# Hybrid decoder step: half tiles of the gated unit and the third head unit change places in the head recurrence

## The chip, the cores and the metric

One core of one Trainium2 chip runs the kernel, one inference step of a small decoder. The metric is device time in microseconds (us), the median of the runs. The engines are TensorE (PE: matmuls; PEld is its loading of weights), VectorE (DVE), ScalarE (ACT), GpSimd (POOL) and SyncE (SP). SP and POOL issue the transfers; SP's queue streams the weights into a ring of seven slots.

## What is computed

Two layers. Each projects its normalized input, runs two token mixers beside each other, merges them and ends in a feed-forward part: dense in the first layer, a mixture of eight experts in the second. The change lies in the mixers:

```python
# branch A: diagonal complex scan y, then a gated linear unit
out = (y @ w_glu1) * jax.nn.sigmoid(y @ w_glu2)
# branch B: for 8 heads, a matrix state s over the tokens
def step(s, inp):
    r_t, w_t, k_t, v_t, kk_t, a_t = inp
    sa = jnp.einsum('bhvk,bhk->bhv', s, -kk_t)
    s = (s * w_t[:, :, None, :] + sa[..., None] * (kk_t * a_t)[:, :, None, :]
         + v_t[..., None] * k_t[:, :, None, :])
    return s, jnp.einsum('bhvk,bhk->bhv', s, r_t)
# merge, then the feed-forward part
m = sigmoid(g_a) * A + sigmoid(g_b) * B
x = x + m @ w_out
```

There are 272 prompt tokens (one sequence) and 8 single-token samples with a state of their own.

## The kernel before

All activations lie with features on the partitions, 280 columns (272 prompt tokens, 8 samples). The recurrence of branch B isn't run token by token: the prompt is cut into a first piece of 16 tokens (the "head" steps, names with s_) and four chunks of 64. A **unit** is a pair of chunks for half of the heads: units 0 and 1 serve chunks 0 and 1, units 2 and 3 chunks 2 and 3. A unit's steps run in a fixed order: gram, square, quad_, oct_, e8, m_, m2, q_, inv. They build the inverse of a 64x64 triangular matrix per head by repeated squaring; each is a set of 64x64 products on PE into two PSUM banks of the unit's own (2u and 2u + 1), read out by ACT or DVE before the next step can start. When both units of a pair are done, the **chunk steps** follow, one chunk after the other: chunk_in (product with the state at the chunk's start), a DVE addition, chunk_solve (product with the inverse), a copy on ACT and one on DVE, chunk_state (the new state), a DVE addition. Then outputs(l, 0) or outputs(l, 1) makes the outputs of the pair.

The **samples** need one step of the recurrence: samples_in (128 products with two columns each), samples_rows (rows into two banks, turned), samples_dot, then samples_spread on DVE and samples_state on PE and DVE, one for each of four head pairs.

The **gated unit** has 8 tiles of 128 features. A tile n is a gate half, glu_half(l, n, 1), with a sigmoid on ACT (glu_gate), and a value half, glu_half(l, n, 0); DVE multiplies both into the merge gate (glu_out). A half is four 128x128 products with 280 columns into bank 4 (the first gate half: bank 5). The half tiles don't depend on the recurrence and stand between its steps.

The order is written out by hand, three times: rwkv(l) of the tensor engine (L914), of ACT (L1482) and of DVE (L2102). Each engine works through its list, with semaphore waits inside the steps. The lists start with the gated unit's first half tiles and units 0 and 1; unit 3 starts beside their end; unit 2 starts at gram(l, 2), between the steps of the first pair's chunks (it waits until all eight tiles of the gated unit are done, because its banks are 4 and 5). The last six half tiles (tiles 5, 6, 7) stand ahead of chunk_state(l, 0).

finish_rwkv(l) (L1005) waits until both pairs' outputs (o_out) and the samples' states (so_out) are done, gives seven ring slots back to SP, and normalizes the outputs; from there on the layer is a chain up to the feed-forward part. POOL stores the samples' states when so_out has reached its last count.

Names in the code: pools[i] is PSUM bank i; room(l, u, i) a buffer of unit u; mm (L447) issues every matmul, fn (L1282) every ACT operation, so the profile's lines for these two engines are always the same, and steps are told apart by shape, count and time. Of DVE's lines, L2047 is chunk_in, L2053 chunk_solve, L2059 chunk_state, L2066 outputs, L2011 the additions of the unit steps, L2093 samples_spread, L2099 samples_state, L1937 and L1939 glu_out.

## Time and profile before

| | us |
|---|---|
| median of 3 runs | 2017.32 |
| lowest and highest | 2012.21, 2017.56 |
| the profiled execution, its own time | 2021.26 |
| span in the profile | 2019.5 |
| PE busy | 1931.4 (96%) |
| DVE busy | 1342.5 (66%) |
| ACT busy | 978.1 (48%) |

The profile is of one execution. Busy shares are means over stages with different limits: the experts, the last half of the span, are dense on PE, while the mixers have stretches in which PE waits. A row of the timeline gives start, length, engine, line, operation, operands (out<-in, with buffers by name: "arena", "ring" and "s" are SBUF, "bank" is PSUM), the count of merged instructions, and in brackets the idle time before and what ended it. The ends of matmuls are modelled, so two neighbouring rows can overlap; starts are exact. A product in 32-bit floats is two matmul instructions. The granted clock is a share of 2.4 GHz, the higher of two levels; the lower is 1.2 GHz.

For the two layers, the stage between the change's first and last step is cut into A (six half tiles among unit steps), a short stretch around chunk_in(0), C (unit and chunk steps without half tiles), D (from the samples' products to the end of unit 2) and E (the second pair's chunks, up to the first sums of finish_rwkv).

### The profile page before, as it was taken

To read this page: it belongs to the slowest core of one execution; us is meant where nothing else is said; L and a number is where in the kernel's file an instruction comes from. 1 tells how busy PE (TensorE), PEld (TensorE's weight loads), DVE (VectorE), ACT (ScalarE), POOL (GpSimd) and SP (SyncE) were. 2 spreads that over 40 slices of the span, in tenths; PEclk is the share of its full clock that TensorE was granted. 3 is DMA by queue.
4 is the path that set the end of the run, shared out by engine and by line. 5 is a ranking of instruction groups with operands and counts; after the bars stand their busy time and mean duration, and the time that the engine had idled before them with its cause. 6 is when DMAs were issued, how large, how long until landed. Compare 5 with 4: busy or idle time off the path is not lost.

```text
span 2019.5 us, 34327 instructions
## 1 busy us (share of the span) xinstructions
PE 1931.4 (96%) x14001; PEld 1600.4 (79%) x14001; DVE 1342.5 (66%) x1479; ACT 978.1 (48%) x957; POOL 44.9 (2%) x40
## 2 busy tenths in 40 slices
PE   8999998899999999998699999999999999999997
PEld 6876885799987777876588787887878878788775
DVE  7484344445534384353478888988888888888885
ACT  2232321344321213220377767768677776767763
POOL 0000000000000000000000000000000000000000
PEclk9989997999999899988699999999999999999998
DMA  8534005344443451015299999999999999999982
GB/s 333 140 67 89 2 3 211 137 172 175 174 139 112 106 97 54 2 57 198 85 346 378 356 377 353 365 380 358 371 366 372 367 362 377 360 368 365 407 333 86
DMA packets 69949, 474.75 MB, mean 235 GB/s; under 512 B 8721, under 2 KB 9905, under 8 KB 14617
## 3 DMA queue, kind: packets, MB, share of 16 engines
q1 hardware_dynamic: 64800, 451.33, 60.3%
q0 software_dynamic: 4736, 20.74, 3.7%
q8 instruction: 86, 1.41, 0.3%
q10 hardware_dynamic: 304, 1.08, 0.1%
q14 instruction: 23, 0.18, 0.0%
HBM read 463.92 MB, written 11.37 MB: 235 GB/s over the span
## 4 chain that ended last, share of the span: by engine, by line
PE 46%; ACT 2%; DVE 1%; DMA 1%; issue 1%; DVEq 0%; ACTq 0%; SPq 0%
PE bank L447 44%; ACT w_hi L1282 1%; PE bank L1235 1%; DMA ring<-wstream_dram 1%; PE bank L1161 0%; ACT he_hi L1282 0%; DVE he_lo L2297 0%; DVE w_lo L2344 0%; DMA arena<-tokens_dram,token_i 0%; PE bank L1171 0%; DVE arena L2291 0%; DVE arena L1687 0%; DVE x L2310 0%; DVE rstd L1685 0%; DVE y_lo L2304 0%
## 5 line engine op out<-in xcount | busy, mean ns | idle before, releaser
L2344 DVE TENSOR_TENSOR w_lo<-ring,w_hi 128x2048 fp32r<-128x2048 f32 x336 | 754.9, 2284 | 42.4 <-ACT w_hi L1282 41.1
L1282 ACT ACTIVATE w_hi<-ring 128x2048 fp32r<-128x2048 f32 x336 | 626.1, 1911 | 38.7 <-DMA ring<-wstream_dram 37.9
L447 PE MATMUL bank<-arena,ring 128*128 128x280 f32 (+1 forms) x1856 | 441.8, 401 | 18.9 <-DVE arena L1914 7.9
L447 PEld LDWEIGHTS bank<-arena,ring 128*128 128x128 f32 (+1 forms) x1856 | 341.4, 195 | 105.0 <-issue 21.4
L1282 ACT ACTIVATE arena<-bank 128x280 f32<-128x280 f32 (+8 forms) x292 | 131.7, 468 | 583.3 <-PE bank L447 550.3
L447 PE MATMUL bank<-w_hi,he_hi 128*128 128x512 f32 x896 | 361.8, 404 | 9.0 <-DVE he_lo L2297 8.5
L447 PE MATMUL bank<-w_lo,he_hi 128*128 128x512 f32 x896 | 354.1, 395 | 0.0
L447 PE MATMUL bank<-w_hi,he_lo 128*128 128x512 f32 x896 | 353.4, 394 | 0.0
L447 PEld LDWEIGHTS bank<-w_hi,he_hi 128*128 128x128 f32 x896 | 169.0, 189 | 50.2 <-issue 11.9
L447 PEld LDWEIGHTS bank<-w_hi,he_lo 128*128 128x128 f32 x896 | 168.9, 189 | 41.4
L447 PEld LDWEIGHTS bank<-w_lo,he_hi 128*128 128x128 f32 x896 | 169.4, 189 | 35.9
L447 PE MATMUL bank<-w_hi,at_hi 128*128 128x512 f32 x448 | 177.8, 397 | 0.4 <-DVE w_lo L2344 0.4
L447 PE MATMUL bank<-w_hi,at_lo 128*128 128x512 f32 x448 | 177.0, 395 | 0.0
L447 PE MATMUL bank<-w_lo,at_hi 128*128 128x512 f32 x448 | 175.2, 391 | 0.0
L447 PE MATMUL bank<-arena 64*64 64x64 f32 (+14 forms) x3920 | 160.4, 250 | 11.5 <-ACT arena L1282 5.4
L447 PEld LDWEIGHTS bank<-arena 64*64 64x64 f32 (+7 forms) x3920 | 135.2, 142 | 38.0 <-issue 19.0
L1680 DVE TENSOR_TENSOR w_lo<-ring,fw_hi 128x2048 fp32r<-128x2048 f32 x33 | 75.6, 2292 | 51.2 <-ACT fw_hi L1282 51.2
L447 PE MATMUL bank<-h_hi,fw_hi 128*128 128x280 f32 x352 | 104.0, 295 | 5.1 <-DVE h_lo L2182 5.1
L447 PE MATMUL bank<-h_lo,fw_hi 128*128 128x280 f32 x352 | 103.5, 294 | 0.0
L447 PE MATMUL bank<-h_hi,w_lo 128*128 128x280 f32 x352 | 103.3, 293 | 0.0
L447 PEld LDWEIGHTS bank<-w_hi,at_lo 128*128 128x128 f32 x448 | 84.1, 188 | 19.5
L447 PEld LDWEIGHTS bank<-w_lo,at_hi 128*128 128x128 f32 x448 | 84.3, 188 | 19.2
(276 smaller groups left out, 1783.4 us busy)
## 6 DMA issues: line engine op xcount, KB each, us to landing
ring<-wstream_dram SPq DMA_DIRECT2D x427, 1024.0 KB, 6.7
parts_dram<-zeros_dram POOLq DMA_DIRECT2D x1, 2112.0 KB, 14.0
s<-s_dram POOLq DMA_DIRECT2D x2, 1024.0 KB, 14.4
o_rw_dram<-s POOLq DMA_DIRECT2D x2, 1024.0 KB, 4.9
arena<-parts_dram POOLq DMA_DIRECT2D x2, 1024.0 KB, 11.7
x<-x_dram SPq DMA_DIRECT2D x2, 560.0 KB, 4.3
y_dram<-arena SPq DMA_DIRECT2D x4, 280.0 KB, 2.1
arena<-s_b_dram POOLq DMA_DIRECT2D x2, 512.0 KB, 6.3
```

The source lines that it names most:

```text
L447: return nc.tensor.matmul(out, lhsT, rhs, start=start, stop=stop, **k)
L1235: last = nc.tensor.transpose(pools[2][:, b * P:(b + 1) * P], act_e[:, b * P:(b + 1) * P], ident[:])
L1282: return nc.scalar.activation(out, in_, func, **k)
L1680: v.tensor_tensor(w_lo[(FFN_AT + n) % RING], slot(FFN_AT + n), fw_hi[n % 4].bitcast(F32), ALU.subtract)\
L2344: v.tensor_tensor(w_lo[n % RING], slot(n), w_hi[n % HALVES].bitcast(F32), ALU.subtract)\
```

## The change

The third unit (unit 2) starts earlier, beside unit 3, with its steps between those of unit 3 and the first pair's chunks. The last six half tiles of the gated unit go behind: between the chunk steps of the second pair. Since unit 2 uses bank 4 before they run, they go to bank 3, and the first of them waits until ACT has read outputs(l, 0) out of that bank. samples_rows then can't use bank 3 and runs in two parts through bank 1, the second part after ACT has read the first. The last two samples_state steps go behind outputs(l, 1). gram(l, 2) waits for five tiles of the gated unit, not eight. On DVE the decay of the samples' states is cut into two halves. The number of products and of elementwise operations is the same.

```diff
@@ -61,2 +61,3 @@
 HELD = 4
+GLU_LATE = 5
 
@@ -327,2 +328,5 @@
 
+        def glu_bank(n, c):
+            return 3 if n >= GLU_LATE else 5 if n == 0 and c else 4
+
         def quad(bank, n):
@@ -567,5 +571,7 @@
                 s = MIX_AT[l] + S_WIN + n // 2
-                bank = 5 if n == 0 and c else 4
+                bank = glu_bank(n, c)
                 if n == 0 and c:
                     pe.wait_ge(S["bonus_out"], l + 1)
+                if n == GLU_LATE and c:
+                    pe.wait_ge(S["o_act"], 4 * l + 2)
                 if c:
@@ -709,3 +715,3 @@
                     pe.wait_ge(S["tok_out"], 6 * l + 6)
-                    pe.wait_ge(S["glu_out"], DC * (l + 1))
+                    pe.wait_ge(S["glu_out"], DC * l + GLU_LATE)
                 if u_ == 3:
@@ -884,10 +890,13 @@
 
-            def samples_rows(l):
+            def samples_rows(l, i):
 
-                pe.wait_ge(S["sm_out"], l + 1)
-                pe.wait_ge(S["o_act"], 4 * l + 2)
-                for j, (bank, row) in enumerate(((1, 0), (1, 32), (3, 0), (3, 32))):
+                if i == 0:
+                    pe.wait_ge(S["sm_out"], l + 1)
+                    pe.wait_ge(S["o_act"], 4 * l + 2)
+                else:
+                    pe.wait_ge(S["smt_out"], 2 * l + 1)
+                for j, row in enumerate((0, 32)):
                     for f in range(CB):
-                        src = (sm[:, f, :, 0], z[:, 8 + f, TP:T], beta_e[:, f, TP:T], chi_e[:, f, TP:T])[j]
-                        last = mm(pools[bank][row:row + NS, f * P:(f + 1) * P], src, ident[:])
+                        src = (sm[:, f, :, 0], z[:, 8 + f, TP:T], beta_e[:, f, TP:T], chi_e[:, f, TP:T])[2 * i + j]
+                        last = mm(pools[1][row:row + NS, f * P:(f + 1) * P], src, ident[:])
                 last.then_inc(S["smt_ps"], 1)
@@ -903,3 +912,3 @@
                 if f == 0:
-                    pe.wait_ge(S["smt_out"], l + 1)
+                    pe.wait_ge(S["smt_out"], 2 * l + 2)
                 elif f == 1:
@@ -952,53 +961,54 @@
                 token_rows(l, 1, 1)
-                glu_half(l, 5, 1)
                 m_(l, 1)
                 m2(l, 0)
-                quad_(l, 3)
                 token_rows(l, 1, 2)
-                glu_half(l, 5, 0)
+                quad_(l, 3)
                 m2(l, 1)
                 q_(l, 0)
+                gram(l, 2)
                 oct_(l, 3)
-                glu_half(l, 6, 1)
                 q_(l, 1)
                 inv(l, 0)
+                square(l, 2)
                 e8(l, 3)
-                glu_half(l, 6, 0)
                 inv(l, 1)
+                quad_(l, 2)
                 m_(l, 3)
-                glu_half(l, 7, 1)
                 chunk_in(l, 0)
+                oct_(l, 2)
                 m2(l, 3)
-                glu_half(l, 7, 0)
                 chunk_solve(l, 0)
+                e8(l, 2)
                 q_(l, 3)
-                gram(l, 2)
                 chunk_state(l, 0)
+                m_(l, 2)
                 inv(l, 3)
                 chunk_in(l, 1)
-                square(l, 2)
-                chunk_solve(l, 1)
-                quad_(l, 2)
-                chunk_state(l, 1)
-                oct_(l, 2)
-                outputs(l, 0)
-                e8(l, 2)
-                samples_in(l)
-                m_(l, 2)
-                samples_rows(l)
                 m2(l, 2)
-                samples_dot(l)
+                chunk_solve(l, 1)
                 q_(l, 2)
+                chunk_state(l, 1)
                 inv(l, 2)
-                samples_state(l, 0)
+                outputs(l, 0)
                 chunk_in(l, 2)
-                samples_state(l, 1)
+                samples_in(l)
+                glu_half(l, 5, 1)
                 chunk_solve(l, 2)
-                samples_state(l, 2)
+                glu_half(l, 5, 0)
                 chunk_state(l, 2)
+                samples_rows(l, 0)
+                glu_half(l, 6, 1)
                 chunk_in(l, 3)
-                samples_state(l, 3)
+                samples_dot(l)
+                samples_rows(l, 1)
+                glu_half(l, 6, 0)
                 chunk_solve(l, 3)
+                glu_half(l, 7, 1)
+                samples_state(l, 0)
                 chunk_state(l, 3)
+                glu_half(l, 7, 0)
+                samples_state(l, 1)
                 outputs(l, 1)
+                samples_state(l, 2)
+                samples_state(l, 3)
 
@@ -1408,3 +1418,3 @@
                 ac.wait_ge(S["glu_ps"], DC * l + n + 1)
-                fn(glu_s[:, n % 2, :], pools[4 if n else 5][:, 0:T], ACT.Sigmoid).then_inc(S["glu_sig"], 1)
+                fn(glu_s[:, n % 2, :], pools[glu_bank(n, 1)][:, 0:T], ACT.Sigmoid).then_inc(S["glu_sig"], 1)
 
@@ -1473,8 +1483,8 @@
 
-            def samples_rows(l):
-                ac.wait_ge(S["smt_ps"], l + 1)
+            def samples_rows(l, i):
+                ac.wait_ge(S["smt_ps"], 2 * l + i + 1)
                 ac.wait_ge(S["smt_zero"], l + 1)
-                for bank, out in ((1, out_r(l)), (3, out_l)):
-                    for row in (0, 32):
-                        ins = fn(out[row:row + NS], pools[bank][row:row + NS, :].rearrange("p (f a v) -> p f a v", f=CB, a=2), ACT.Identity)
+                out = (out_r(l), out_l)[i]
+                for row in (0, 32):
+                    ins = fn(out[row:row + NS], pools[1][row:row + NS, :].rearrange("p (f a v) -> p f a v", f=CB, a=2), ACT.Identity)
                 ins.then_inc(S["smt_out"], 1)
@@ -1509,29 +1519,30 @@
                 token_rows(l, 1, 1)
-                glu_gate(l, 5)
                 m_(l, 1)
-                quad_(l, 3)
                 token_rows(l, 1, 2)
+                quad_(l, 3)
                 q_(l, 0)
                 oct_(l, 3)
-                glu_gate(l, 6)
                 q_(l, 1)
                 inv(l, 0)
+                square(l, 2)
                 inv(l, 1)
+                quad_(l, 2)
                 m_(l, 3)
-                glu_gate(l, 7)
+                oct_(l, 2)
                 chunk_solve(l, 0)
                 q_(l, 3)
+                m_(l, 2)
                 inv(l, 3)
-                square(l, 2)
                 chunk_solve(l, 1)
-                quad_(l, 2)
-                oct_(l, 2)
-                outputs(l, 0)
-                samples_in(l)
-                m_(l, 2)
-                samples_rows(l)
                 q_(l, 2)
                 inv(l, 2)
+                outputs(l, 0)
+                samples_in(l)
+                glu_gate(l, 5)
                 chunk_solve(l, 2)
+                samples_rows(l, 0)
+                glu_gate(l, 6)
+                samples_rows(l, 1)
                 chunk_solve(l, 3)
+                glu_gate(l, 7)
                 outputs(l, 1)
@@ -1938,3 +1949,3 @@
                 dve.wait_ge(S["glu_value_ps"], DC * l + n + 1)
-                v.tensor_tensor(gate[:, n, :], gate[:, n, :], pools[4][:, 0:T], ALU.mult).then_inc(S["glu_out"], 1)
+                v.tensor_tensor(gate[:, n, :], gate[:, n, :], pools[glu_bank(n, 0)][:, 0:T], ALU.mult).then_inc(S["glu_out"], 1)
 
@@ -2073,4 +2084,7 @@
                 tt(sm_r[:, 1], chi_e[:, :, TP:T], z[:, 0:4, TP:T], ALU.mult).then_inc(S["sm_dot_in"], 1)
+
+            def samples_decayed(l, fs):
+                tt = v.tensor_tensor
                 dve.wait_ge(S["sm_ps"], l + 1)
-                for f in range(CB):
+                for f in fs:
                     tt(s0[:, f], s0[:, f], wend[:, f, 1 + NCH:].unsqueeze(2).broadcast_to([P, NS, N]), ALU.mult)
@@ -2088,3 +2102,3 @@
             def samples_spread(l, f):
-                dve.wait_ge(S["smt_out"], l + 1)
+                dve.wait_ge(S["smt_out"], 2 * l + 1)
                 if f >= 2:
@@ -2125,5 +2139,5 @@
                 quad_(l, 3)
-                glu_out(l, 5)
                 m2(l, 1)
                 q_(l, 0)
+                gram(l, 2)
                 oct_(l, 3)
@@ -2131,38 +2145,40 @@
                 e8(l, 3)
-                glu_out(l, 6)
+                quad_(l, 2)
                 m_(l, 3)
                 chunk_in(l, 0)
+                oct_(l, 2)
                 m2(l, 3)
-                glu_out(l, 7)
                 chunk_solve(l, 0)
+                e8(l, 2)
                 q_(l, 3)
-                gram(l, 2)
                 chunk_state(l, 0)
+                m_(l, 2)
                 chunk_in(l, 1)
+                m2(l, 2)
                 chunk_solve(l, 1)
-                quad_(l, 2)
+                q_(l, 2)
                 chunk_state(l, 1)
-                oct_(l, 2)
-                e8(l, 2)
                 outputs(l, 0)
-                m_(l, 2)
                 samples_ready(l)
-                m2(l, 2)
-                samples_dot(l)
-                q_(l, 2)
+                chunk_in(l, 2)
+                samples_decayed(l, (0, 1))
+                chunk_solve(l, 2)
+                glu_out(l, 5)
+                chunk_state(l, 2)
+                samples_decayed(l, (2, 3))
                 samples_spread(l, 0)
+                chunk_in(l, 3)
+                samples_dot(l)
                 samples_spread(l, 1)
+                glu_out(l, 6)
+                chunk_solve(l, 3)
                 samples_state(l, 0)
-                chunk_in(l, 2)
                 samples_spread(l, 2)
+                chunk_state(l, 3)
+                glu_out(l, 7)
                 samples_state(l, 1)
-                chunk_solve(l, 2)
                 samples_spread(l, 3)
-                chunk_state(l, 2)
+                outputs(l, 1)
                 samples_state(l, 2)
-                chunk_in(l, 3)
                 samples_state(l, 3)
-                chunk_solve(l, 3)
-                chunk_state(l, 3)
-                outputs(l, 1)
```

## Rows read from the trace of the kernel before

**Rows 1.** Windows, layer 0: stretch, busy time by engine, granted clock, DMA share, GB/s.
```profile
243.58:266.05 22.47, 22.47 (x399) 18.97 (x398) 6.83 (x17) 5.99 (x13) 0.00 (x0) 1.00 0.01 2
...
270.02:284.31 14.29, 13.50 (x415) 13.29 (x415) 6.67 (x17) 3.18 (x8) 0.00 (x0) 1.00 0.01 3
...
284.31:299.88 15.57, 14.72 (x299) 13.23 (x295) 8.10 (x22) 4.51 (x10) 0.00 (x0) 0.78 0.01 2
...
299.88:316.57 16.69, 14.44 (x240) 10.90 (x240) 10.21 (x20) 2.23 (x5) 1.45 (x2) 0.80 0.21 74
```

**Rows 2.** The windows view, layer 1: the last three of the same stretches.
```profile
857.44:871.73 14.29, 13.50 (x414) 13.29 (x415) 6.67 (x17) 3.18 (x8) 0.00 (x0) 1.00 0.01 3
...
871.73:885.58 13.85, 13.05 (x300) 11.32 (x296) 8.29 (x22) 4.51 (x10) 0.00 (x0) 0.88 0.02 4
...
885.58:903.33 17.75, 15.47 (x241) 12.26 (x241) 10.23 (x20) 2.27 (x5) 1.45 (x2) 0.71 0.20 68
```

**Rows 3.** Waits of weight loads, D and E: us, times, longest; both layers.
```profile
PEld bank L447 <- DVE arena L2047: 2.2, 2, 1.2
...
PEld bank L447 <- DVE ring L2093: 0.8, 2, 0.6
...
PEld bank L447 <- DVE ring L2059: 0.7, 1, 0.7
...
PEld bank L447 <- DVE arena L2011: 0.6, 2, 0.4
...
PEld bank L447 <- DVE arena L2047: 1.9, 2, 1.0
...
PEld bank L447 <- DVE arena L2011: 0.4, 1, 0.4
```

**Rows 4.** The same view of A to C, layer 0.
```profile
PEld bank L447 <- DVE ring L2059: 0.9, 1, 0.9
```

**Rows 5.** Windows of 5 us around the samples' products, both layers.
```profile
280.00:285.00 5.00, 5.00 (x188) 5.00 (x182) 1.76 (x5) 1.39 (x4) 0.00 (x0) 1.00 0.01 3
...
285.00:290.00 5.00, 5.00 (x119) 5.00 (x118) 0.77 (x2) 0.04 (x1) 0.00 (x0) 0.63 0.01 3
...
875.00:880.00 5.00, 5.00 (x93) 4.13 (x93) 2.42 (x7) 0.82 (x2) 0.00 (x0) 0.68 0.02 3
```

**Rows 6.** The timeline of PE: start, length, operation, count, idle before.
```profile
243.69 2.05 PE L447 MATMUL bank<-arena,ring 128*128 128x280 f32 x8
...
818.54 3.84 PE L447 MATMUL bank<-arena,ring 128*128 128x280 f32 x8
...
284.45 5.15 PE L447 MATMUL bank<-arena,s 64*64 64x2 f32 x122
...
871.88 3.76 PE L447 MATMUL bank<-arena,s 64*64 64x2 f32 x123
```

**Rows 7.** The timeline of ACT, layer 0: reads of chunk_solve(3) and of outputs(1).
```profile
309.99 0.38 ACT L1282 ACTIVATE arena<-bank 64x256 f32<-64x256 f32 x1 [6.03 <-PE bank L447]
...
315.08 0.66 ACT L1282 ACTIVATE arena<-bank 128x256 f32<-128x256 f32 x2 [4.71 <-PE bank L447]
```

**Rows 8.** Timeline: sigmoid of the sixth gate half; product with its value half.
```profile
245.84 0.40 ACT L1282 ACTIVATE arena<-bank 128x280 f32<-128x280 f32 x1 [1.35 <-PE bank L447]
...
252.60 0.45 DVE L1939 TENSOR_TENSOR arena<-arena,bank 128x280 f32<-128x280 f32 x1 [1.68 <-PE bank L447]
```

**Rows 9.** The timeline around the end of the stage, layer 0.
```profile
308.49 0.69 DVE L2099 TENSOR_TENSOR s<-s,bank 128x512 f32<-128x512 f32 x1 [0.56 <-PE bank L447]
...
315.77 0.69 DVE L2066 TENSOR_TENSOR arena<-arena,bank 128x512 f32<-128x512 f32 x1 [3.63 <-ACT arena L1282]
...
316.60 4.46 PE L447 MATMUL bank<-arena,blk 128*128 128x280 f32 x14 [1.57 <-DVE arena L2066]
...
329.87 17.40 PE L447 MATMUL bank<-arena,ring 128*128 128x280 f32 x64 [3.97 <-DVE arena L1914]
```

**Rows 10.** The page, part 6: one DMA issue.
```profile
o_rw_dram<-s POOLq DMA_DIRECT2D x2, 1024.0 KB, 4.9
```

44 lines of the change are left out of this document (22 added, 22 removed).

## The prediction

> **What bounds the kernel now.** The edit touches one stage only, the head recurrence, once in each of the two layers. I cut that stage into stretches with the windows view and asked of each how long it is, how busy TensorE (PE) is and which clock it is granted [rows 1, 2]. The reader is to see three things. In the first stretch (A, with six half tiles of the gated unit between the unit steps) PE never rests and the granted clock is 1.00, that is 2.4 GHz. In C (unit and chunk steps alone) it is still 1.00, with a short rest. In D and E (samples, then the second pair of chunks) the mean granted clock falls to 0.78 and 0.80 in layer 0 and to 0.88 and 0.71 in layer 1. So the stage is bound by PE's own program order: the timeline shows its steps one behind the other as rwkv writes them, and what PE waits for, or does at 1.2 GHz, is paid in full.
>
> Next I read the waits of PE's weight loads, which start at the moment a wait ends and so show stalls that the modelled ends of matmuls cover [rows 3, 4]. In D and E named waits are 2.2 + 0.8 + 0.7 + 0.6 = 4.3 us in layer 0 and 1.9 + 0.8 + 0.7 + 0.4 = 3.8 us in layer 1 (the two rows at 0.8 and 0.7 read the same there), all for VectorE (DVE): chunk 2 and chunk 3 are a chain of chunk_in, solve and state with a DVE or ScalarE (ACT) step after each, and the order gives PE next to nothing to do between them. In A to C there is one such wait, 0.9 us, in front of the second chunk. The "issue" waits of at most 0.3 us are the ordinary change from one kind of step to another, and stay.
>
> Third, the clock. The first fall comes with the samples' products (64x2): PE is busy 5.00 of 5.00 us both in the slice before and in the slice in which the clock drops to 0.63, and layer 1 shows the same at 0.68 [rows 5]. So it isn't idleness that brings this fall. The second fall is in E, where PE stops and starts between the chunk steps. What the lower level does to a step is seen in like rows: a half tile takes 2.05 us at 2.4 GHz and 3.84 at 1.2, and the samples' products 3.76 and 5.15, the latter only partly at the lower level [rows 6].
>
> **The change, part by part.** All PE work is kept: the same half tiles, unit steps, chunk steps and sample products. What changes is what lies between what.
>
> *Six half tiles leave A, unit 2 takes their place.* This costs nothing if each unit step still has cover for its hand-over. A hand-over is about 0.1 us from the last product to the reader and 0.4 for the reader [rows 8], estimated at 0.5 to 0.8 in all with wider reads. Products of the 64x64 kind go at the rate of 3.76 us for 123, or 31 ns [rows 6], so a step of 32 to 48 covers 1.0 to 1.5 us. In the new order nearly every step of units 2 and 3 has at least 32 products of other work before its successor; the tightest are square(2) to quad_(2) (behind e8(3) and inv(1)) and m_(2) to m2(2) (behind inv(3) and chunk_in(1)), 32 products each, and m2(2) to q_(2), behind the 16 of chunk_solve(1) alone. I take 0.4 us of stalls a layer; the bounds are 0 and the whole of the cover gone (a rival, below). The 0.9 us wait in front of chunk_in(1) goes: it came from five DVE operations of gram(2) queued ahead of chunk_state(0), and gram(2) now lies long before.
>
> *Six half tiles go between the second pair's chunk steps.* Each is 2.05 us, and the longest wait there is 1.2. So the named waits of D and E go, with unit 2's own (q_ and inv behind DVE) since unit 2 is done earlier. Recovered: 0.9 + 4.3 = 5.2 us in layer 0, 0.9 + 3.8 = 4.7 in layer 1, 9.9 in all.
>
> *The second fall of the clock.* In E the time at 1.2 GHz is 2 x 0.20 x 16.69 = 6.7 us in layer 0 and 2 x 0.29 x 17.75 = 10.3 in layer 1. At most half of what isn't waiting in it is lost: (6.7 - 1.2) / 2 = 2.7 and (10.3 - 1.6) / 2 = 4.4. From below: chunk_state(3) and outputs(1), 128 products, lie between two ACT reads 5.09 us apart, against 128 x 31 ns = 3.9, a loss of 1.2 [rows 7], and layer 1 at least as much, estimated 1.4. Dense half tiles now stand between these steps and the rests are gone, as in A where the level was 1.00, so I count the loss as recovered: the middle of the bounds, 1.9 and 2.9, together 4.8 us; bounds 2.6 and 7.1.
>
> *The first fall stays.* The samples' products still run 128 in a row. In D the fall costs (1 - 0.78) x 15.57 = 3.4 us in layer 0 and (1 - 0.88) x 13.85 = 1.7 in layer 1. Afterwards it will hit the half tiles instead of m_(2) and the sample rows, at about the same price; nothing is gained, 5.1 us stay lost.
>
> The Trainium skill ("TensorE: Matmul & The Clock Gate", section "What's actually happening") says that the clock follows how busy PE has lately been, and that idling lowers it. The trace doesn't agree for the samples' products, which lowered it with PE busy throughout; by that rule the new order, with no rests, would not lose these 5.1 us, and the sum would be 1998.1 us.
>
> *Added waits.* The first moved gate half waits for ACT's reads of outputs(0), because it writes bank 3; all later PE work queues behind it. chunk_in(2) and 128 sample products (3.76 us or more) lie between, against a read of 0.66 [rows 7]: nothing. Without that cover it would cost about 0.8. Gate and value half share a bank, so a value half waits for the sigmoid: a half starts at 243.69 and its sigmoid is done at 246.24, 2.55 later [rows 6, 8], but 2.05 of the half itself and a 16-product step or more lie between: nothing, else 0.5 for each of three pairs. A gate half waits for the previous value's product on DVE, 0.45 long, with a chunk or sample step between: nothing.
>
> *DVE's and ACT's own orders* are rewritten to follow PE's; the decay of the samples' states is cut in two halves so that chunk_solve(2) doesn't queue behind all of it. DVE is busy 8.1 + 10.2 of 32.3 us in D and E and ACT 4.5 + 2.2 [rows 1], so the three products with half tiles that move there (two operations of 0.45 each, 2.7 us) find room: nothing, 0.5 us a layer as a bound.
>
> *samples_rows in two parts through one bank* adds a switch, 0.3 us, and its second part waits for ACT's two reads of the first, behind a half tile and chunk_in(3): nothing.
>
> *The end.* Two samples_state steps move behind outputs(1). Before, the sums of finish_rwkv start 1.5 us after ACT's read of outputs(1) (315.08 to 316.60), by way of a DVE addition of 0.69 [rows 9]. Now two DVE additions of 0.69 (samples_state 2 and 3) queue behind that addition on DVE, in program order, and finish_rwkv waits for them too: 1.4 us more. In return two PE steps of about 0.9 (estimated as two 512-column products at the lower rate of a 128-row gate half) leave the path in front of outputs(1): -1.8. Net -0.4.
>
> *Other queues.* SP's refill of the seven held ring slots is released at the same place, at finish_rwkv's start, and the next weights are needed only at 329.87, where PE waits for DVE and not for a DMA, 13.3 us later [rows 9]. POOL's store of the samples' states (1024 KB, 4.9 us [rows 10]) now starts together with that refill instead of before it; if it held the first slot back by its whole length, 13.3 us still cover it: nothing. Nothing else in POOL's queue waits on the moved steps. What follows the stage is a chain without slack that starts earlier by what is won.
>
> **How the numbers follow.** Gain: 9.9 (waits) + 4.8 (second fall) - 0.8 (stalls, two layers) - 0.6 (switch) + 0.8 (end) = 14.1 us. The profiled execution took 2021.26 us by its own time (span 2019.5, so 1.8 around it), which gives 2007.2; it is 3.9 above the median of the runs, 2017.32, so the same gain from the median gives 2003.2. The runs shown differ by 5 us among themselves; 0.3% (6 us) is about what a measurement of this kernel can tell from no change.
>
> **The rivals.**
> 1. Forecast: waits and second fall go, first fall stays: 2003.2, own range 1999 to 2007 from the bounds of the second fall (2.6 to 7.1) and stalls up to 2 us. Chance 0.44.
> 2. No fall at all: dense half tiles on both sides of the samples' products hold the clock at 2.4 GHz. For it: A is at 1.00 with small steps among half tiles. Against it: the fall comes inside or right behind the samples' products in both layers, whatever follows. 2003.2 - 5.1 = 1998.1. Chance 0.15.
> 3. The second fall stays or another takes its place (sample rows of 8 columns, the last outputs), while the waits go: 2003.2 + 4.8 = 2008.0. Chance 0.25.
> 4. It doesn't do what it says: the waits only move, because unit 2 and unit 3 side by side lack the half tiles' cover (their chains are nine hand-overs each, and DVE has five operations of gram(2) in their way). 2003.2 + 9.9 = 2013.1. Against it: C runs such steps side by side with one 0.9 us wait. Chance 0.10.
> 5. Slower: the stretch without half tiles becomes long, and small products alone let the clock fall to 1.2 GHz. The stretch is 284.31 - 243.58 = 40.7, less six halves (12.3), plus unit 2's last 128 products (3.9), less 0.9: 31.4 us a layer. C shows 14.3 us of such work at 1.00 [rows 1, 2]; the other 17.1 a layer are untried. All of them at 1.2 GHz cost 17.1 each: 2003.2 + 34.2 = 2037.4. It turns the gain into a loss from 14.1 us lost, or some 7 of the 17.1 a layer. Chance 0.06.
>
> Eight times in ten: from 1996.0 (case 2 with 2.1 to spare for the runs' spread) to 2010.0 (case 3 with 2.0), which leaves out most of 4 and all of 5. Faster by over 0.3%: 0.83 (cases 1 and 2, most of 3, a little of 4); within 0.3%: 0.11; slower: 0.06.
>
> **What would show it.** Right: in the windows of the changed kernel the stage is some 7 us shorter in each layer; no weight load between the second pair's steps waits for DVE's L2047 and L2059 lines; the granted clock is 1.00 until the samples' products, falls once there, and is 1.00 again through the chunk steps with half tiles. Stalls in front of quad_(2) or m2(2) over 0.5 us would make the cover claim wrong, a clock below 1.00 before the samples' products would make case 5 right, and a late bo product (waiting for a DMA) the claim on SP's queue wrong.

## The result, and the profile after

| | before | after |
|---|---|---|
| median, us (4 runs each) | 2015.8 | 1998.41 |
| range of the runs, us | 2012.21 to 2017.56 | 1997.21 to 2001.71 |
| profiled execution: own time / span, us | 2021.26 / 2019.5 | 2001.71 / 1999.9 |
| mean granted clock | 0.96 | 0.97 |

The ratio is 0.9908 (95% interval 0.9889 to 0.9927): faster by 0.7 to 1.1%. The forecast was 2003.2, its range 1996 to 2010. The two profiled executions differ by 19.55 us, where 14.1 were forecast; where these lie is read below.

The windows view of after, both layers. Stretches: unit and chunk steps without half tiles; the samples' products to the first sum of finish_rwkv (layer 0 also in three parts); and from that sum to the first bo product. Columns as in [rows 1].

```profile
243.96:275.31 31.35, 30.57 (x965) 30.03 (x965) 15.63 (x40) 9.59 (x22) 0.00 (x0) 1.00 0.02 4
...
275.31:311.65 36.34, 35.00 (x443) 26.38 (x440) 18.96 (x41) 7.31 (x16) 0.00 (x0) 0.86 0.01 2
...
275.31:289.20 13.89, 13.73 (x168) 11.22 (x165) 4.53 (x11) 1.63 (x5) 0.00 (x0) 0.63 0.01 2
289.20:296.50 7.30, 7.30 (x92) 5.34 (x90) 5.30 (x14) 1.58 (x3) 0.00 (x0) 1.00 0.01 2
296.50:311.65 15.15, 13.97 (x186) 9.82 (x185) 9.13 (x17) 4.10 (x8) 0.00 (x0) 1.00 0.01 2
311.65:322.79 11.14, 4.58 (x24) 2.48 (x25) 8.68 (x19) 2.24 (x5) 1.48 (x2) 0.87 0.88 334
...
824.40:855.69 31.29, 30.51 (x967) 29.97 (x966) 15.63 (x40) 9.64 (x22) 0.00 (x0) 1.00 0.02 4
855.69:888.40 32.71, 31.54 (x443) 23.97 (x440) 18.96 (x41) 7.26 (x16) 0.00 (x0) 0.95 0.01 2
888.40:899.54 11.14, 4.58 (x24) 2.47 (x25) 8.69 (x19) 2.24 (x5) 1.48 (x2) 0.87 0.88 327
```

The same view of before, from the first sum to the first bo product, which was not among the rows that the prediction rested on:

```profile
316.57:329.87 13.30, 6.46 (x24) 3.30 (x25) 8.68 (x19) 2.91 (x7) 0.00 (x0) 0.64 0.91 373
903.33:916.23 12.90, 6.34 (x24) 3.08 (x25) 8.68 (x19) 2.87 (x7) 0.00 (x0) 0.66 0.91 367
```

From the end of token_rows(1, 1), where A begins [rows 1], to the first sum, the stage took 73.0 and 72.3 us before (from 243.58 and 831.00) and takes 67.7 (243.96 to 311.65) and 64.0 (824.40 to 888.40) now: 5.3 and 8.3 shorter, 13.6 in all, against 14.1 forecast. The next stage is 2.2 and 1.8 shorter, 3.9 in all, which nothing in the forecast had. The remaining 2.0 lie in stages that the edit doesn't touch (2.9 less behind layer 1's bo product, 0.9 more elsewhere). The clock answers to [rows 1, 2, 5]: the first fall is still there, in layer 0 even longer, and the second, in the stretch that was E, is gone. In 5 us slices of after:

```profile
275.00:280.00 5.00, 4.84 (x152) 4.75 (x145) 2.46 (x7) 0.66 (x2) 0.00 (x0) 0.89 0.03 7
280.00:285.00 5.00, 5.00 (x18) 3.47 (x19) 1.29 (x2) 0.63 (x2) 0.00 (x0) 0.50 0.00 0
285.00:290.00 5.00, 5.00 (x32) 3.73 (x32) 1.02 (x3) 0.38 (x1) 0.00 (x0) 0.59 0.00 0
...
860.00:865.00 5.00, 5.00 (x27) 3.75 (x27) 1.77 (x4) 0.83 (x3) 0.00 (x0) 0.75 0.02 3
```

In the second row PE runs a half tile and then chunk_solve(2) without a rest, and yet the granted clock stays at 0.50 (1.2 GHz): that half tile, from 280.03, takes 4.10 us, one from 292.07 takes 2.15.

The waits of weight loads in after, which answer to [rows 3, 4]: first the stretch without half tiles, then that from the samples' products to the sum, both of layer 0.

```profile
PEld bank L451 <- issue: 1.2, 2, 1.0
...
PEld bank L451 <- issue: 6.0, 13, 2.0
PEld bank L451 <- DVE ring L2107: 0.4, 1, 0.4
```

Every wait of [rows 3, 4] on DVE is gone. The 0.4 is no such wait, whatever its name: it stands at 305.22 ahead of samples_state(1), 0.37 long as behind other half tiles, and the spread that this step needs was done at 297.6. The 2.0 of "issue" at the end is the wait for finish_rwkv's inputs, seen on PE below. The 1.0 in the first row is new. The timeline there, PE and then ACT (start, length, operation, count, idle before):

```profile
243.57 0.66 PE L745 MATMUL bank<-ident,arena 128*128 128x128 f32 x4
245.00 0.68 PE L451 MATMUL bank<-ring 64*64 64x64 f32 x16 [0.78 <-ACT arena L1292]
```

```profile
243.69 1.17 ACT L1292 ACTIVATE arena<-bank 128x512 f32<-128x512 f32 x2 [0.34 <-PE bank L451]
```

m_(1) waits for ACT's read of token_rows(1, 1), which glu_half(5, 1) used to cover. The end of the stage, which answers to [rows 9]: ACT's read of outputs(1), DVE's addition and the two moved ones, the first sum.

```profile
308.98 0.66 ACT L1292 ACTIVATE arena<-bank 128x256 f32<-128x256 f32 x2 [6.62 <-PE bank L451]
```

```profile
309.67 0.69 DVE L2077 TENSOR_TENSOR arena<-arena,bank 128x512 f32<-128x512 f32 x1 [1.43 <-ACT arena L1292]
310.27 1.28 DVE L2113 TENSOR_TENSOR s<-s,bank 128x512 f32<-128x512 f32 x2
```

```profile
311.65 1.65 PE L451 MATMUL bank<-arena,blk 128*128 128x280 f32 x6 [1.18 <-DVE s L2113]
```

From read to sum 2.67 us, 1.15 more than the 1.52 of before. The bo product still waits for DVE, and for no DMA, though the states' store, which now runs beside the refill, takes 12.4 us instead of 4.9 [rows 10]. The waits view from the sums on, and the page's part 6:

```profile
PE bank L451 <- DVE arena L1925: 4.0, 1, 4.0
```

```profile
o_rw_dram<-s POOLq DMA_DIRECT2D x2, 1024.0 KB, 12.4
```

### The profile page after: what moved, and what is told of

Read it like the earlier page. It is cut to its first block, busy times and chain, and to the rows that moved or that the text cites. A ratio compares the mean times of both kernels' runs of the same rounds, so it can differ in the third digit from the quotient of the medians.

```text
span 1999.9 us, 34329 instructions
## 1 busy us (share of the span) xinstructions
PE 1912.3 (96%) x14001; PEld 1587.2 (79%) x14001; DVE 1343.5 (67%) x1479; ACT 976.8 (49%) x957; POOL 45.0 (2%) x40
## 4 chain that ended last, share of the span: by engine, by line
PE 48%; ACT 2%; DVE 1%; issue 1%; DMA 0%; DVEq 0%; ACTq 0%
PE bank L451 46%; PE bank L1245 1%; ACT w_hi L1292 1%; PE bank L1171 0%; DVE he_lo L2313 0%; ACT he_hi L1292 0%; DMA arena<-tokens_dram,token_i 0%; PE bank L1181 0%; DVE arena L2307 0%; DVE arena L1698 0%; DVE w_lo L2360 0%; DVE x L2326 0%; DVE rstd L1696 0%; DVE y_lo L2320 0%; DVE arena L2331 0%
## 5 line engine op out<-in xcount | busy, mean ns | idle before, releaser
L451 PE MATMUL bank<-arena 64*64 64x64 f32 (+14 forms) x3920 | 152.7, 246 | 12.4 <-ACT arena L1292 5.4
L451 PEld LDWEIGHTS bank<-arena 64*64 64x64 f32 (+7 forms) x3920 | 128.3, 138 | 35.2 <-issue 20.6
## 6 DMA issues: line engine op xcount, KB each, us to landing
o_rw_dram<-s POOLq DMA_DIRECT2D x2, 1024.0 KB, 12.4
arena<-parts_dram POOLq DMA_DIRECT2D x2, 1024.0 KB, 11.7
```

The costliest lines, as they stand in the source:

```text
L451: return nc.tensor.matmul(out, lhsT, rhs, start=start, stop=stop, **k)
```

## The experiments

Each edit is made in the changed kernel, unless it says otherwise. "Tail" is the windows row from the samples' first product (half_ahead: from the half tile in front of it) to the first sum, "next" the time from there to the first bo product. Where the edit leaves other work inside the tail, its row says so. "Ratio" is to the kernel before, timed beside each; its 95% interval is some 0.001 to 0.004 to either side. Products are counted as in the prediction, by matmul instructions: the samples' 128 are 64 products of two instructions each.

| kernel | median, us | ratio | tail, layer 0 / 1, us | clock in it | next, us |
|---|---|---|---|---|---|
| changed kernel | 1998.41 | 0.9908 | 36.34 / 32.71 | 0.86 / 0.95 | 11.1 / 11.1 |
| after_again | 1994.22 | 0.9884 | 32.98 / 35.88 | 0.95 / 0.86 | 11.2 / 11.2 |
| rows_early | 1993.51 | 0.9872 | 34.23 / 32.70 | 0.90 / 0.95 | 11.2 / 11.2 |
| end_back | 2005.26 | 0.9937 | 36.33 / 35.74 | 0.91 / 0.89 | 13.0 / 13.5 |
| end_ready | 1997.98 | 0.9903 | 33.56 / 33.49 | 0.95 / 0.95 | 12.6 / 11.2 |
| halves_alone (unit 2's late steps in it too) | 2010.57 | 0.9967 | 41.39 / 39.81 | 0.92 / 0.96 | 11.7 / 11.7 |
| half_ahead | 1995.81, two runs | 0.9892 | 34.20 / 34.20 | 0.90 / 0.90 | 11.7 / 11.2 |
| samples_cut | 1992.98 | 0.9889 | 31.06 / 31.07 | 1.00 / 1.00 | 11.2 / 11.2 |
| cut_and_early | 1994.45 | 0.9881 | 34.30 / 32.75 | 0.90 / 0.95 | 11.2 / 11.2 |
| all_three | 1996.11 | 0.9889 | 34.81 / 34.90 | 0.90 / 0.90 | 11.2 / 12.4 |
| samples_four | 1992.96 | 0.988 | 33.43 / 31.78 | 0.95 / 1.00 | 12.7 / 12.8 |
| samples_quarter (96 products a layer left out) | 1985.33, one run | | 28.47 / 28.38 | 1.00 / 0.99 | 11.2 / 12.6 |

The kernel before had medians of 2017.2 to 2018.8 beside these, and single runs from 2011.4 to 2025.7.

**after_again: the changed kernel once more.**

> The changed kernel as it is, once more, beside the others of this row. Theory: the fall behind the samples' products comes in each layer again (spells of 3 to 10 us at 1.2 GHz, not always as long), none in the end of the stage or among the sums of finish_rwkv ahead of the idle time at the bo product; 1997 to 2000 us. Rival: the falls are a matter of chance from run to run, and another profile of the same kernel shows none, or one in the end of the stage: then the differences of single profiles say little, and only the medians count.

Windows, both layers:

```profile
275.47:308.45 32.98, 31.75 (x443) 24.08 (x439) 18.95 (x41) 7.26 (x16) 0.00 (x0) 0.95 0.01 2
845.98:881.86 35.88, 34.74 (x443) 26.09 (x439) 18.95 (x41) 7.26 (x16) 0.00 (x0) 0.86 0.01 2
```

The long fall is now in layer 1 and the short one in layer 0, the other way round than in the first profile. That there is a fall behind the samples' products is the kernel's; how long it is changes from one execution to the next. The same kernel's two medians, 1998.41 and 1994.22, differ by 4.2 us for that and like reasons, so edits worth 1 or 2 us are read from stretches below, not from medians. All its four runs lie below the median of the first set, and their median below the 1997 to 2000 expected here and below the forecast's range (1996 to 2010): the time forecast is missed on the side of too little gain.

**samples_cut: the samples' products in two runs, a half tile between.** (glu_gate(5) goes ahead of samples_in on ACT, too.)

```
-                samples_in(l)
+                samples_in(l, 0)
                 glu_half(l, 5, 1)
+                samples_in(l, 1)
```

> The 128 products of samples_in (64x2 each) are cut into two runs of 64, and the half tile glu_half(5, 1) stands between them; nothing else moves. Theory: what lowers TensorE's clock in the stage is the unbroken run of two-column products, so with the run cut the fall near 279 us (10.2 us at 1.2 GHz in layer 0 of the changed kernel) and near 859 us (3.4 us) goes or gets shorter; the stage gets shorter by up to 5.0 us in layer 0 and 1.4 us in layer 1, 1992 to 1996 us in all. Rival: the fall belongs to the place (whatever follows 30 us of small products), and cutting the run changes nothing: a spell at 1.2 GHz of the same length within some us of the same place, and 1998 us. Second rival: the two halves of the run bring one fall each, and the time is 1998 to 2003 us.

```profile
273.68:304.74 31.06, 29.91 (x443) 22.77 (x440) 18.86 (x41) 7.27 (x16) 0.00 (x0) 1.00 0.01 3
842.42:873.49 31.07, 29.92 (x443) 22.78 (x440) 18.86 (x41) 7.27 (x16) 0.00 (x0) 1.00 0.01 2
```

No fall in either layer, and two tails that agree to 0.01 us. This is the tail at 2.4 GHz, and it gives the price of the falls: 36.34 - 31.06 = 5.3 us and 32.71 - 31.07 = 1.6 in the changed kernel. It looked as if the theory were right; the next two say otherwise. (The profiled execution is the fastest of its four runs, which go from 1986.66 to 1998.25.)

**cut_and_early and all_three: the cut again, with other edits.** Both put token_rows(1, 1) ahead of m_(0); all_three also moves samples_state(0) to (2) forward (and, on DVE, the spread of (3) ahead of glu_out(7)):

```
-                glu_half(l, 7, 1)
                 samples_state(l, 0)
+                glu_half(l, 7, 1)
                 chunk_state(l, 3)
-                glu_half(l, 7, 0)
                 samples_state(l, 1)
-                outputs(l, 1)
+                glu_half(l, 7, 0)
                 samples_state(l, 2)
+                outputs(l, 1)
                 samples_state(l, 3)
```

> Two edits together: samples_in cut in two by glu_half(5, 1), and token_rows(1, 1) ahead of m_(0). Theory: they hit different places and add up. From the first product of token_rows(1, 0) to that of m_(1) 6.0 us, as with the early rows alone (6.82 in the changed kernel); no fall of the clock between the samples' products and the end of the stage; from the first product of s_gram to the first sum of finish_rwkv 108.2 us in each layer (108.98 with the cut alone, 114.3 and 110.6 in the changed kernel); 1988 to 1992 us in all. Rival: the fall went by chance in the one profile with the cut run, and comes back here: stage 110 to 113 us in one layer or both, 1994 us or more.

> As the run with the cut samples_in and the early token_rows(1, 1), and besides the steps samples_state(0) to (2) and glu_half(7, 1), (7, 0) change places, so that samples_state(2) stands ahead of outputs(1) and only (3) behind it; the samples' spread of (3) comes ahead of glu_out(7) on VectorE. Theory: one VectorE addition less stands between ScalarE's read of outputs(1) and the first sum (2.67 us in the changed kernel, 2.0 here), a gain of 0.6 us a layer, if samples_state(2) doesn't have to wait for its spread on VectorE (with both steps ahead TensorE waited 2.4 us for it, and the clock fell behind that): with the last half tile between, a wait of at most 0.4. The stage is 0.3 to 0.6 us shorter than with the two other edits. Rival: VectorE's spread is late here too, TensorE waits 1 us or more ahead of outputs(1), and the end of the stage or the stage behind it falls to 1.2 GHz: 2 to 6 us longer.

Windows of cut_and_early, both layers:

```profile
275.11:309.41 34.30, 33.16 (x443) 24.61 (x439) 18.86 (x41) 7.27 (x16) 0.00 (x0) 0.90 0.01 2
850.84:883.59 32.75, 31.60 (x443) 23.84 (x440) 18.87 (x41) 7.27 (x16) 0.00 (x0) 0.95 0.01 2
```

The same PE work as in samples_cut, and the fall is back in both layers; so it is in both of all_three (0.90 and 0.90). With all products in one run, the 8 profiles taken (before and after_again among them) show the fall in both layers, 16 of 16; with the run cut in two, 4 of 6. The cut makes it less certain at best. In 3 of these 4 layers it is two falls, one right behind each half of the run (cut_and_early, layer 0: at 277.56 and 284.38, 3.4 us each; all_three: at 279.25 and 286.07, 856.10 and 862.93), as the second rival of samples_cut has it, though not its time. In all_three the last samples_state steps don't wait for the spread either, but its tail at a clock of 0.90 is no shorter than that of cut_and_early at 0.90.

**half_ahead: the half tile in front of the samples' products, the run whole.**

> The run of 128 two-column products stays whole, and only changes places with the half tile: glu_half(5, 1) ahead of samples_in, not behind or within it. With the run cut in two by that half tile the fall of TensorE's clock was gone in both layers, and the stage fell from 70.5 and 66.9 us (first product of m_(0) to the first sum of finish_rwkv) to 65.2 and 65.2. Theory: it is the length of the run that lowers the clock, so with the run whole a fall comes back within some us of its start, in both layers, and the stage is 67 to 71 us. Rival: what mattered is that a dense half tile stands ahead of (some of) the products; then there is no fall here either and the stage is 65 to 66 us (chunk_in(2) alone covers ScalarE's read for the half tile, some 0.3 us may be waited for).

Both tails are 34.20 us at a clock of 0.90: a fall in both layers. A dense half tile right ahead doesn't prevent it, and one right behind doesn't end it at once (the 5 us slices above).

**samples_quarter and before_quarter: 32 of the 128 products, in the changed kernel and in the one before.**

```
-                for f in range(CB):
+                for f in range(1):
```

> The changed kernel with only the first quarter of the samples' products: 32 of the 128 products with two columns in each layer, the other 96 left out (the samples' outputs lack them). So far every profile with the run whole shows a fall of TensorE's clock 2.5 to 4 us after the run's start, in both layers, and of three kernels with the run cut in two one shows none and two show it. Theory: the two-column products bring it; with 32 left the clock stays at 1.00 from the start of the stage to the idle time at the bo product, and from m_(0) to the first sum of finish_rwkv the stage takes 62 us in each layer (65.2 us in the profile without a fall, less 96 products of 31 ns). Rival: the fall comes at the end of the long stretch of small products, whatever they are; it comes here too, within some us of the same place (275 to 282 us and 846 to 859 us), and costs 1.5 to 5 us in at least one layer.

> The kernel before with only the first quarter of the samples' products, as in the run beside it, 96 two-column products left out in each layer. Theory: the first fall (286.3 us and 876.8 us, 2 to 5 us behind the run's start) goes here as well, while the second one (306.8 and 890.4 us), which comes where TensorE waits between the chunk steps of the second pair, stays: two falls less, about 3.0 us a layer for the products and 1.7 to 3.4 us a layer for the clock, 2006 to 2010 us. Rival: the first fall stays or moves into the next steps; 2010 to 2013 us.

Windows of samples_quarter: the tails of both layers.

```profile
273.93:302.40 28.47, 27.24 (x347) 20.02 (x343) 18.87 (x41) 7.32 (x16) 0.00 (x0) 1.00 0.01 2
840.12:868.50 28.38, 27.24 (x345) 20.02 (x341) 18.86 (x41) 7.22 (x16) 0.00 (x0) 0.99 0.01 2
```

The first fall is gone in both layers, and the tail is shorter than samples_cut's by 2.6 and 2.7 us, most of what 96 products cost (3.0). So it is the number of these products, and not the place, that decides: the same 30 us of small products stand ahead of it here. Windows of before_quarter, layer 0:

```profile
283.06:289.00 5.94, 5.94 (x148) 5.37 (x146) 4.16 (x10) 2.31 (x6) 0.00 (x0) 1.00 0.01 3
289.00:295.50 6.50, 5.30 (x84) 3.24 (x79) 6.43 (x18) 2.19 (x5) 0.00 (x0) 1.00 0.01 3
295.50:309.20 13.70, 13.13 (x172) 11.14 (x174) 7.14 (x14) 0.76 (x2) 1.45 (x2) 0.50 0.20 74
```

In the old order the fall at the samples is gone as well, but one of 13.7 us comes where PE is idle for 1.2 of 6.5 us between the chunk steps (layer 1: 882.6, 17.1 us). In before there were two of 6.8 (layer 1: 3.4 and 10.2). So the samples' products aren't the only thing that brings a fall, and in the old order a later one takes what the first gives up: one run of 2011.09 us, above the theory's 2006 to 2010 and at the near end of the rival's range. That PE's rests bring the later one is argued from its place. In the new order, with half tiles between the chunk steps, nothing takes it between the samples and the end of the stage. The pair differs in the whole change, so it shows that the new order holds the clock there; which part of it does is read from halves_alone below. It doesn't hold to the last: in layer 1 of samples_quarter the clock falls at 868.0, right at the sums, and "next" is 12.6 instead of 11.2.

**samples_four: all products, in four runs of 32.** (token_rows(1, 1) stands ahead of m_(0) here, too; ACT's and DVE's orders follow.)

```
-                samples_in(l)
+                samples_in(l, 0)
                 glu_half(l, 5, 1)
+                samples_in(l, 1)
                 chunk_solve(l, 2)
+                samples_in(l, 2)
                 glu_half(l, 5, 0)
+                samples_in(l, 3)
                 chunk_state(l, 2)
-                samples_rows(l, 0)
                 glu_half(l, 6, 1)
+                samples_rows(l, 0)
```

> All 128 two-column products of the samples are kept, but in four runs of 32 with other work between: glu_half(5, 1), chunk_solve(2) and glu_half(5, 0); samples_rows(0) and the first half of the decay on VectorE move one step back, and token_rows(1, 1) stands ahead of m_(0). With 32 of the products left and 96 left out, both falls behind the samples were gone (stage 62.7 and 62.6 us from m_(0) to the first sum). Theory: it is many two-column products close together that lower the clock; spread over 10 us they don't, and the stage is 65.7 us by that count (62.7 and the 96 products of 31 ns), that is 1988 to 1992 us in all, the shortest of the kernels with all the work. Rival: their number and not their closeness counts, and a fall comes behind the third or fourth run in at least one layer: 67 to 70 us there, 1993 to 1998 us in all.

```profile
275.03:308.46 33.43, 31.61 (x443) 23.86 (x440) 18.86 (x41) 7.26 (x16) 0.00 (x0) 0.95 0.01 2
849.95:881.73 31.78, 29.96 (x443) 22.76 (x439) 18.86 (x41) 7.25 (x16) 0.00 (x0) 1.00 0.01 2
```

A fall in one layer, right behind the third run as the rival has it, and none in the other: neither theory. And in both layers the clock now falls at the first sum, so that "next" is 12.7 and 12.8. What was won at the samples was lost there. The median, 1992.96, has a ratio of 0.988 (0.9856 to 0.9904) to before; after_again has 0.9884 (0.9859 to 0.9909). No kernel here beats the changed one by more than the intervals.

**rows_early: token_rows(1, 1) one step earlier.** (On ACT as well.)

```
+                token_rows(l, 1, 1)
                 m_(l, 0)
                 square(l, 3)
-                token_rows(l, 1, 1)
                 m_(l, 1)
```

> token_rows(1, 1) stands one step earlier, ahead of m_(0), on TensorE and ScalarE. In the changed kernel the first product of m_(1) starts 1.13 us after the last weight load of token_rows(1, 1), in both layers, with no half tile left between them. Theory: m_(1) waits for ScalarE's read of token_rows(1, 1), which the moved glu_half(5, 1) used to hide; with m_(0) and square(3) between (80 products, 2.4 us) the wait goes and the stage gets 0.9 to 1.0 us shorter in each layer, 1996.5 us in all, less than these runs scatter, so it is read in the trace. Rival: the 1.13 us are the wait of m_(1) for VectorE's steps (oct_(1) and e8(1)), and stay where they are: the stage is as long as in the changed kernel, 1998.4 us.

The waits view of 240 to 276.4 us, layer 0 (in the changed kernel it has 1.5, 3, 1.0 from 240 to 275.3):

```profile
PEld bank L451 <- issue: 0.7, 3, 0.4
```

The 1.0 wait is gone, and from the first weight load of token_rows(1, 0) to that of m_(1) there are 6.00 us (240.16 to 246.16, 815.86 to 821.86) instead of 6.82 (238.15 to 244.97, 818.59 to 825.41): 0.82 a layer, the theory's wait and a little under its size. The rival falls.

**end_back: samples_state(2) and (3) ahead of outputs(1) again.** (On DVE as well.)

```
                 samples_state(l, 1)
-                outputs(l, 1)
                 samples_state(l, 2)
                 samples_state(l, 3)
+                outputs(l, 1)
```

> One part undone: samples_state(2) and (3) stand ahead of outputs(1) again, on TensorE and VectorE; all else is as in the changed kernel. Theory: behind outputs(1) the two VectorE additions of 0.69 us each stand between ScalarE's read and the first sum of finish_rwkv (2.67 us from read to sum in the changed kernel, 1.52 before), so undone the stretch from the read to the sum is 1.5 us again; but the two steps now stand ahead of outputs(1) on TensorE, and the stage as a whole is 0 to 0.4 us longer in each layer. Rival: TensorE's part of the two steps is hidden between half tiles and chunk steps either way, and undoing the move wins 1.1 us in each layer, 1996 us in all.

Weight-load waits of the tail, layer 0; PE's timeline at samples_state(3) and the first sum; windows of layer 0 around the end.

```profile
PEld bank L451 <- DVE ring L2107: 2.4, 2, 2.0
```

```profile
302.96 0.65 PE L451 MATMUL bank<-ring,arena 40*64 40x512 f32 x2 [1.13 <-DVE ring L2107]
...
308.24 1.51 PE L451 MATMUL bank<-arena,blk 128*128 128x280 f32 x4 [1.57 <-DVE arena L2077]
```

```profile
299.00:303.00 4.00, 2.87 (x16) 0.95 (x14) 3.58 (x8) 0.00 (x0) 0.00 (x0) 1.00 0.01 2
303.00:308.20 5.20, 3.67 (x100) 2.95 (x100) 1.88 (x3) 1.47 (x3) 1.48 (x2) 1.00 0.37 134
...
309.00:312.40 3.40, 3.40 (x12) 1.69 (x10) 2.08 (x6) 1.58 (x4) 0.00 (x0) 0.50 1.01 329
```

The stretch from read to sum is 1.5 us again (306.71 to 308.24), as the theory said. But the rival's sign is wrong and the theory's size (0 to 0.4 us a layer): undoing it costs 6.9 us against the first median of the changed kernel and 11.0 against the second (by the ratios 6 and 11; the interval, 0.9914 to 0.9961, overlaps with the first one's, 0.9889 to 0.9927, and not with the second's, 0.9859 to 0.9909). Of the 2.4 us, 0.4 is the step behind a half tile again; 2.0 is samples_state(3) waiting for DVE's spread, for which it doesn't wait behind outputs(1). TensorE is idle for 1.1 of 4.0 and 1.5 of 5.2 us; and the clock falls among the sums (layer 1 already at 885.8, ahead of them), so that "next" is 13.0 and 13.5.

**end_ready: the four steps ahead of outputs(1), the spread in time.** (PE's order at the end: samples_state(0), glu_half(7, 1), chunk_state(3), samples_state(1), glu_half(7, 0), samples_state(2), (3), outputs(1); DVE makes the spread of (3) ahead of glu_out(7).)

> All four samples_state steps ahead of outputs(1), as in the run that put (2) and (3) back, but with the samples' spread done in time: samples_state(0) and (1) stand one slot earlier, so that VectorE makes the spread of (3) ahead of glu_out(7). In the run with (2) and (3) back, TensorE waited 2.4 us for the spread and the clock fell to 1.2 GHz among the sums of finish_rwkv. Theory: the wait and the idle time cost it, not the order as such. Here TensorE waits less than 0.6 us ahead of outputs(1), the clock is 1.00 among the sums, from ScalarE's read of outputs(1) to the first sum 1.5 us (2.67 in the changed kernel); the stage is 0.5 to 1.2 us shorter than in the changed kernel at like clock, 1993 to 1997 us in all. Rival: it is the two steps behind outputs(1) that keep TensorE busy while ScalarE and VectorE read, and with them ahead of it the clock falls among the sums again, with 2 us lost there in each layer: 1997 to 2004 us.

Windows, the tails of both layers and "next" of layer 0:

```profile
272.59:306.15 33.56, 32.02 (x443) 23.71 (x439) 19.22 (x41) 6.60 (x15) 1.48 (x2) 0.95 0.06 23
...
845.43:878.92 33.49, 31.95 (x443) 23.55 (x440) 19.22 (x41) 6.59 (x15) 1.48 (x2) 0.95 0.06 21
...
306.15:318.74 12.59, 6.02 (x25) 2.77 (x25) 8.69 (x19) 2.91 (x7) 0.00 (x0) 0.67 1.00 396
```

No wait for the spread is left (the row has the 0.4), as forecast, and the read leads to the sum in 1.5 us. Yet the tails are 0.5 to 0.9 us longer than the two of the changed kernel at the same 0.95 (32.71 and 32.98), so the second addition saved behind the read buys nothing; and the clock falls among the sums in layer 0 and not in layer 1. The wait for the spread costs its 2.0 us; the fall at the sums came in 1 of 2 layers without it and in 2 of 2 with it, too few to tell more.

**halves_alone: the half tiles moved, unit 2 left at its old place.** (All samples_state steps stand ahead of outputs(1) again, too; ACT's and DVE's orders follow.)

```
-                gram(l, 2)
                 oct_(l, 3)
                 q_(l, 1)
                 inv(l, 0)
-                square(l, 2)
...
                 samples_in(l)
                 glu_half(l, 5, 1)
-                chunk_solve(l, 2)
+                m_(l, 2)
+                samples_rows(l, 0)
                 glu_half(l, 5, 0)
-                chunk_state(l, 2)
...
+                m2(l, 2)
```

> One part alone: the six half tiles are moved behind outputs(0), as in the changed kernel, but the third unit (unit 2) keeps its old place, its late steps among samples and half tiles. Theory: both parts are needed. Units 0, 1 and 3 lose the cover of the half tiles and have no unit 2 beside them, so waits of 0.5 to 1 us each show in front of m2, q_ and inv; chunk_in(3), chunk_solve(3), chunk_state(3) and outputs(1) come last with nothing between them, with waits of 0.7 and 0.6 us as before and small products at the lower clock. The stage is 4 to 7 us longer than in the changed kernel in each layer: 2007 to 2012 us. Rival: the half tiles alone bring it (they fill the waits of the second pair and hold the clock), and unit 2's place is worth nothing: 1998 to 2000 us.

The waits of weight loads: the stretch ahead of the samples, then the tail, layer 0.

```profile
PEld bank L451 <- DVE ring L2070: 0.9, 1, 0.9
PEld bank L451 <- ACT arena L1292: 0.4, 1, 0.4
PEld bank L451 <- DVE arena L2022: 0.3, 1, 0.3
...
PEld bank L451 <- DVE arena L2058: 0.9, 1, 0.9
PEld bank L451 <- ACT arena L1292: 0.8, 2, 0.5
PEld bank L451 <- DVE ring L2070: 0.7, 1, 0.7
```

4.0 us of named waits where the changed kernel has the 0.4, and 2010.57 us (ratio to before 0.9967, 0.9953 to 0.998). The theory is right in the size and in the waits: of the 17 to 23 us that the change brings, the half tiles alone bring 7 to 8; the rest came only with unit 2 ahead of them. Unit 2 moved alone wasn't run. In one point the theory is wrong: it expected the last chunk steps at the lower clock. The windows of layer 0, from behind the last half tile to the first sum:

```profile
305.00:308.00 3.00, 2.46 (x44) 1.45 (x39) 2.56 (x6) 0.00 (x0) 0.00 (x0) 1.00 0.00 0
308.00:311.00 3.00, 2.85 (x93) 2.75 (x93) 1.05 (x3) 0.38 (x1) 1.06 (x2) 1.00 0.41 154
311.00:313.90 2.90, 1.38 (x54) 1.24 (x50) 0.69 (x1) 1.46 (x3) 0.39 (x1) 1.00 0.74 251
```

In the last 16.65 us ahead of the sum PE is busy for 14.45, as in the E of before (14.44 of 16.69 [rows 1]), and the granted clock is 1.00 (0.80 there); layer 1 has 14.45 of 16.70 at 1.00. The second fall is gone here, in both layers of this one profile, with the rests still in place, so it doesn't take the end of the rests to be rid of it. Of the parts of the change that leaves the half tiles; how they do it isn't shown.

## Why the prediction was right, and where not

**The time: in the range, in part by luck.** 1998.41 lies in it, the same kernel's 1994.22 lies 1.8 below. The second rival's 1998.1 is nearer to the first than the forecast's 2003.2, and yet its mechanism, no fall at all, didn't come: the number alone would have picked the wrong one. That the stage came out at 13.6 for 14.1 is in part the work of misses that cancel: the new wait and the dearer first fall cost 2.6 more than the sum had, and 2.2 came back that it didn't have, most of it untraced (below). By layer its terms give 6.8 and 7.3; measured are 5.3 and 8.3.

**Waits (9.9): right, less one that was missed.** The waits of [rows 3, 4] are gone, so 9.9 came back. The step "six half tiles leave A" asked only whether each unit step still covers its hand-over to the next, and left out token_rows, whose reader is ACT: m_(1) now waits, 0.82 us a layer by rows_early, twice the 0.4 that the sum had for stalls. The covers that the prediction named as tightest hold: from 248.5 us (layer 1: 828.9) to the samples no two weight loads start more than 0.11 us apart, where a stall of 0.5 would have refuted it. The "issue" waits weren't at most 0.3 in all rows: A to C have 0.4, and layer 1's last stretch has 1.7, the wait ahead of the first sum; no term of the sum rests on it.

**The second fall (4.8): right.** Between the samples' fall and the end of the stage the granted clock is 1.00 in both layers, in both profiles of the changed kernel. That the new order does it is shown by the pair of quarter runs, and halves_alone, with half tiles in place and the rests still there, points to the half tiles. Of "dense half tiles now stand between these steps and the rests are gone" only the first half was needed. The size can only be bounded: no run has the old stage with this fall alone taken out.

**The first fall: right that it stays, a little too cheap.** 5.1 us were to stay lost; 5.3 + 1.6 = 6.9 us were (32.98 - 31.06 = 1.9 and 35.88 - 31.07 = 4.8 in the second profile: 6.7). The rival with no fall at all is refuted for the changed kernel, 4 layers of 4. The rule of the Trainium skill behind it ("TensorE: Matmul & The Clock Gate", section "What's actually happening": the clock follows how busy PE has lately been) agrees with the second fall, where PE idles, and with what end_back shows, but not with halves_alone, where as much idle time brought no fall. With the first the trace doesn't agree, as the prediction had it: the rows read PE as busy, the clock falls, and taking 96 products of two columns away stops it. That busy time in the profile isn't what lowers or holds the clock there is shown; what of such a product does is not.

**The end (+0.8 for both layers): the term that was mis-sized.** The steps were right: 1.15 us more from read to sum, where 1.4 was forecast, in return for two steps that leave the path ahead of outputs(1). But those were priced by PE's own products, 0.9 us each. Their price in the new order is DVE's spread, which is late ahead of outputs(1) and hidden behind it (2.0 us waited against none), and what follows on the clock. Undone, the move costs some 6 to 11 us for both layers, several times the 0.8. With the spread made in time (end_ready, 0.9903) it costs nothing that can be told from noise.

**The next stage (put at nothing): 3.9 us.** "What follows the stage is a chain without slack that starts earlier by what is won" was taken to keep its length. It had two falls of the clock in it, 0.64 and 0.66 granted, and is 11.1 us long where the clock holds through the sums. The 2.2 and 1.8 us are the main part of what the forecast lacked; the rest, 2.0, lies elsewhere and wasn't traced.

**The slower rival is refuted:** 31 us a layer of small products alone run at a granted clock of 1.00, in both layers and both profiles. **Waits that only move** is refuted too, though halves_alone comes close to it. **Added waits, SP's and POOL's queues at nothing:** right; the store takes 7.5 us longer and nobody waits for it.

**What stays open.** First, a remainder: before has 73.0 and 72.3 us from the end of token_rows(1, 1), less 5.3 and 4.6 for its falls by the forecast's own terms, that is 67.7 in both layers; samples_cut, which has no fall, has 62.35. Of these 5.35 us a layer the waits that went (5.2 and 4.7), the new one (-0.8) and the forecast's 0.4 for the end explain 4.8 and 4.3; 0.5 to 1.1 us were not traced to a step. The second fall may hold them: the forecast's upper bounds for it, 2.7 and 4.4, are 0.8 and 1.5 above the middle that is used here. Second, where a fall comes: in several kernels that lose the fall at the samples (samples_four, layer 1 of samples_quarter, all layers of before_quarter) one comes later, in samples_cut none does until PE idles ahead of the bo product. Whether that is a rule or chance can't be told from these few profiles.

## What to carry to other kernels

Price a moved step by whatever it waits for in its new place, the slower engine's preparation included, and look for the reader of every step that loses its cover, also of those that belong to no chain. Where a late stage of the program runs at a lowered clock, an edit ahead of it can change its length: look at its granted clock before taking it as fixed. When independent work is moved between the steps of a dependent chain, ask what covers the steps at its old place: here the half tiles alone brought 7 to 8 of 17 to 23 us, and the rest came with the third unit moved there.

## What the runs showed of the hardware

Behind products of two columns (64x2) TensorE's clock fell to 1.2 GHz with PE read as busy for 4.84 to 5.00 of the 5.00 us ahead of the fall: in every layer with 128 in one run (16 of 16, within the run or up to 1.2 us behind it), in 4 of 6 with a half tile in the middle, in 1 of 2 in four runs of 32, and right behind them in none of 4 with only 32, two of these in the kernel before. After such a fall, a half tile and a chunk step without a rest didn't raise the clock at once: 5.00 us of them ran at 0.50. Rests of some 2.2 us in 17 went with a fall where no half tile stood among the steps (before) and with none where half tiles stood among them (halves_alone). And one and the same kernel had 10.2 and 3.4 us at 1.2 GHz in its two layers in one profile, 3.4 and 10.2 in the other; a median over runs holds such draws, a single profile one of them.
